# The neighbourhood attention's slots in another order on three engines, its bias table by two row tiles, and the head norm's gate moved into the slots

## The reference, cut to what matters

```python
def neighbourhood_attention(q, k, v, k_ctx, v_ctx, rpb, rows):
    # 1024 latent tokens = 16 rows of 64; 8 heads of 64; 256 context keys
    def one_row(r):
        rws = win_rows[r]                                # 8 rows of keys
        bias = rpb[:, drow[None, :, None], dcol[:, None, :]]
        s_loc = einsum(qr, kw) * scale + bias            # 16 columns of keys in each row
        s_ctx = einsum(qr, k_ctx) * scale
        p = softmax(concatenate([s_loc, s_ctx], -1))
        return einsum(p_loc, vw) + einsum(p_ctx, v_ctx)

def combine(o, na, z, dtype):
    g = head_rmsnorm(merge_heads(o), gla_norm, GLA_HEADS)      # 4 heads of 128
    return (concatenate([g, merge_heads(na)], -1) * silu(z)) @ w_out
```

## Time and profile before

| | us |
|---|---|
| median of three executions | 4608.93 |
| the profiled execution, own time | 4611.05 |
| its span (first to last instruction) | 4609.2 |
| of that, `na_block` up to its first transpose | 1909 to 1976 |
| its 32 slots | 1976 to 2255 |
| its output projection and final sums | 2255 to 2390 |
| mean granted TensorE clock over the span | 0.974 |

### The profile page before, as it was taken

How to read it: one execution, slowest core, us unless ns; L and a number is a source line. 1 busy time by engine, 2 the same in 40 slices (tenths; PEclk the granted TensorE clock), 3 DMA queues, 4 the chain that set the end, 5 groups by cost and what they waited for, 6 DMA issues and landing times. The chain is left out here.

```text
span 4609.2 us, 47596 instructions
## 1 busy us (share of the span) xinstructions
PE 4375.6 (95%) x19074; PEld 2605.8 (57%) x19074; DVE 1433.6 (31%) x3514; ACT 950.4 (21%) x1724; POOL 167.7 (4%) x225
## 2 busy tenths in 40 slices
PE   7999998999999999966889999999999989999998
PEld 3676666775547686755544467656544444444444
DVE  2236663663121455244344311111323210000002
ACT  2233332331134111233214311111111000000000
POOL 2000000000000000011011000001000000000000
PEclk9999999999999999888989999999999999999999
DMA  5310003112010111210012111112223011111110
GB/s 223 108 36 7 8 7 72 41 41 92 27 35 28 53 51 53 90 37 17 28 41 63 32 36 44 46 56 83 91 89 112 28 46 37 41 37 37 46 50 37
DMA packets 102226, 242.91 MB, mean 53 GB/s; under 512 B 15089, under 2 KB 43586, under 8 KB 100439
## 3 DMA queue, kind: packets, MB, share of 16 engines
q1 hardware_dynamic: 94968, 221.38, 14.9%
q0 software_dynamic: 5888, 13.25, 1.1%
q10 hardware_dynamic: 1152, 5.24, 0.3%
HBM read 202.78 MB, written 39.34 MB: 53 GB/s over the span
## 5 line engine op out<-in xcount | busy, mean ns | idle before, releaser
L2299 PE MATMUL lat_banks<-sbuf 128*128 128x512 f32 (+2 forms) x2368 | 846.1, 516 | 0.0
L302 PE MATMUL mlp_prod<-sbuf 128*128 128x512 f32 x1792 | 769.3, 592 | 1.5 <-DVE sbuf L375 1.5
L2299 PEld LDWEIGHTS lat_banks<-sbuf 128*128 128x128 f32 x2368 | 428.6, 206 | 377.5 <-issue 374.2
L302 PEld LDWEIGHTS mlp_prod<-sbuf 128*128 128x128 f32 x1792 | 340.4, 190 | 429.8 <-issue 428.1
L1738 PE MATMUL gla_prod<-sbuf 128*128 128x512 f32 (+1 forms) x784 | 321.4, 566 | 0.2 <-ACT sbuf L1860 0.2
L1225 PE MATMUL mls_banks<-sbuf 128*128 128x512 f32 (+1 forms) x768 | 284.3, 525 | 7.4 <-DMA sbuf<-in_l_w_in 6.8
L1738 PEld LDWEIGHTS gla_prod<-sbuf 128*128 128x128 f32 x784 | 148.0, 192 | 154.1 <-issue 146.0
L1225 PEld LDWEIGHTS mls_banks<-sbuf 128*128 128x128 f32 x768 | 144.4, 192 | 124.1 <-issue 109.1
L2519 ACT ACTIVATE sbuf<-lat_banks 128x512 f32<-128x512 f32 (+1 forms) x124 | 72.4, 583 | 680.0 <-PE lat_banks L2299 629.7
L750 PE MATMUL mla_banks<-sbuf 128*128 128x512 f32 (+1 forms) x416 | 176.0, 511 | 0.0
L351 ACT ACTIVATE sbuf<-mlp_prod 128x1024 f32<-128x1024 f32 x32 | 32.8, 1024 | 641.0 <-PE mlp_prod L302 641.0
(11 more groups left out here) (433 smaller groups left out, 5511.4 us busy)
## 6 DMA issues: line engine op xcount, KB each, us to landing
sbuf<-in_l_w_in SPq DMA_DIRECT2D x59, 512.0 KB, 3.9
sbuf<-in_w_in SPq DMA_DIRECT2D x52, 512.0 KB, 3.8
sbuf<-in_w_mlp_in SPq DMA_DIRECT2D x32, 512.0 KB, 3.6
sbuf<-in_w_mlp_out SPq DMA_DIRECT2D x32, 512.0 KB, 3.6
sbuf<-in_l_w_mod SPq DMA_DIRECT2D x12, 1024.0 KB, 11.1
sbuf<-in_l_w_mod SPq DMA_DIRECT2D x24, 512.0 KB, 5.0
scratch_gates<-sbuf SPq DMA_DIRECT2D x48, 256.0 KB, 2.9
sbuf<-scratch_gates SPq DMA_DIRECT2D x8, 1536.0 KB, 6.9
```

Source lines behind the costliest of these rows:

```text
L302: last = nc.tensor.matmul(prod[:, n % NB, o:o + 512], w[:, n % NB, k * P:(k + 1) * P], rhs, start=k == 0, stop=k == KD - 1)
L2299: last = nc.tensor.matmul(dst, lhsT, rhs, start=k == 0, stop=k == KD - 1)
```

## The change

- PE's order in the slots becomes, for each i, `turn(i)` from its third batch on, `scores(i+2)`, `weigh(i-1)`, and the first two batches of `turn(i+1)`. DVE's becomes `bias_max(i+2)`, `outputs(i-1)`, `copy(i+1)`, `inverse(i+1)`; ACT's `copy(i)`, `soft(i+1)`.
- ACT copies batches 0 and 1 of each slot, DVE 2 and 3.
- The table's 64 matmuls run as two row tiles: `hot` and `lhs` lie twice, at partitions 0 to 32 and 64 to 96, and the matmuls of the two go to different banks. There are 8 parts of 8 matmuls.
- `gla_spread` and `gla_gate` go. POOL multiplies `osum` by silu(z) (`gate(j)`, four tensor-tensor operations of 128x1024) after its second edge tile. In slots 8 to 23 (`GATE0`) `weigh` spreads two 128-token factors into free columns of its own bank, and `outputs` multiplies two 128-column pieces of `osum` with them and the gain, in one operation of 128x256.
- The fourth block of z has a place of its own in `H`, and is loaded with the others. The gates no longer stand ahead of the first slots; two of the four `gla_sums` stand behind `scores(0)`.
- `load` goes. `ones`, `ident` and `eps` are loaded at the end of `modulation`'s SP queue, and its small tensors ahead of the weights.

```diff
-            sp.dma_start(cc[:], io["cc"]).then_inc(in_sem, 16)
+            for dst, src in ((cc[:], io["cc"]), (sel[:], io["mod_sel"]), (b[:], io["l0_b_mod"]), (g[:], io["l0_norm"])):
+                sp.dma_start(dst, src).then_inc(in_sem, 16)
             for c in range(NC):
                 if c >= NB:
                     sp.wait_ge(mm_done, c - NB + 1)
                 for h in range(2):
                     sp.dma_start(w[:, c % NB, 4 * h:4 * h + 4, :],
                                  io["l0_w_mod"][(2 * c + h) * P:(2 * c + h + 1) * P, :].rearrange("p (k n) -> p k n", k=4)).then_inc(w_ready[c % NB], 16)
-                if c == 0:
-                    sp.dma_start(sel[:], io["mod_sel"]).then_inc(in_sem, 16)
-                    sp.dma_start(b[:], io["l0_b_mod"]).then_inc(in_sem, 16)
-                    sp.dma_start(g[:], io["l0_norm"]).then_inc(in_sem, 16)
+            for dst, src in ((ones, io["ones"]), (ident, io["ident"]), (eps, io["eps"])):
+                sp.dma_start(dst, src).then_inc(const_in, 16)
+            sp.wait_ge(const_in, 48)
...
+            act.wait_ge(const_in, 48)
             nc.scalar.activation(rcol[:, 0:TT], stat[:, 0:TT], ACT.Sqrt, bias=eps, scale=1.0 / D).then_inc(rooted, 1)
...
+            pe.wait_ge(const_in, 48)
             column_sums(nc, stat, total, ones, range(TT)).then_inc(ssum, 1)
...
-def load(nc, name, pairs):
...
-    on_act = [b in (1, 2) for i, b in batch]
+    on_act = [b < 2 for i, b in batch]
...
+    NO, NW, GATE0 = 8, 3, 8
...
-        hot, osq = early[0:33, 0:8192], early[:, 8192:10240].rearrange("p (a t) -> p a t", a=2)
+        hot = [early[64 * r:64 * r + 33, 0:4096] for r in range(2)]
+        osq = early[:, 4096:6144].rearrange("p (a t) -> p a t", a=2)
...
-        zg = kv[:, 1, 0:3072].rearrange("p (a t) -> p a t", a=3)
+        quarters = lambda a: a.rearrange("p (n t) -> p n t", t=256)
+        zg = [quarters(kv[:, 1, j * NLAT:(j + 1) * NLAT]) for j in range(3)] + [H[:, 0:4, 0:256]]
...
-            sp.dma_start(lhs[:], io["rpb"]).then_inc(hot_in, 16)
-            sp.dma_start(hot, io["rpb_hot"]).then_inc(hot_in, 16)
+            for r in range(2):
+                sp.dma_start(lhs[64 * r:64 * r + 33, :], io["rpb"]).then_inc(hot_in, 16)
+                sp.dma_start(hot[r], io["rpb_hot"][:, 4096 * r:4096 * (r + 1)]).then_inc(hot_in, 16)
             sp.dma_start(gl[:], io["l1_gla_norm"]).then_inc(gl_in, 16)
             load_pair(0)
-            for j in range(3):
-                sp.dma_start(zg[:, j, :], z_dram[j * P:(j + 1) * P, NCTX:T]).then_inc(zg_in[j], 16)
+            for j in range(4):
+                sp.dma_start(zg[j], quarters(z_dram[j * P:(j + 1) * P, NCTX:T])).then_inc(zg_in[j], 16)
             for j in range(4):
                 sp.dma_start(zn[:, j, :], z_dram[(4 + j) * P:(5 + j) * P, NCTX:T]).then_inc(zn_in, 16)
             sp.dma_start(gf[:], io["final_norm"]).then_inc(gf_in, 16)
             sp.dma_start(gm[:], io["g_mem"]).then_inc(gf_in, 16)
             sp.dma_start(mem, io["mem"].rearrange("p (k t) -> p k t", k=KD)).then_inc(mem_in, 16)
-            sp.wait_ge(ygla, 1)
-            sp.dma_start(zg[:, 0, :], z_dram[3 * P:4 * P, NCTX:T]).then_inc(zg_in[3], 16)
             sp.wait_ge(ygla, 4)
...
+            def gate(j):
+                pool.wait_ge(zsil, j + 1)
+                nc.gpsimd.tensor_tensor(quarters(osum[:, j, :]), quarters(osum[:, j, :]), zg[j], ALU.mult).then_inc(ygla, 1)
...
+                    if p == 0 and e == 1:
+                        pool.drain()
+                        for j in range(4):
+                            gate(j)
+                        pool.drain()
...
             def table_part(b):
-                if b >= 4:
-                    pe.wait_ge(*((tab_act, b // 2 - 1) if b % 2 == 0 else (tab_dve, b // 2 - 1)))
+
+                if b >= 2:
+                    pe.wait_ge(tab_act, b - 1)
+                    pe.wait_ge(tab_dve, b - 1)
                 for a in range(4):
                     kk = 4 * b + a
-                    last = nc.tensor.matmul(banks[:, b % 4, a * P:(a + 1) * P], hot[:, kk * P:(kk + 1) * P], lhs[:], start=True, stop=True)
+                    for r in range(2):
+                        last = nc.tensor.matmul(banks[:, 2 * (b % 2) + r, a * P:(a + 1) * P], hot[r][:, kk * P:(kk + 1) * P],
+                                                lhs[64 * r:64 * r + 33, :], start=True, stop=True)
                 last.then_inc(tabled, 1)
-
-            def gla_spread(j):
-                if j == 0:
-                    pe.wait_ge(ginv, 1)
-                else:
-                    pe.wait_ge(ygla, j)
-                for t in range(8):
-                    last = nc.tensor.matmul(banks[:, 4 + t // 4, (t % 4) * P:(t % 4 + 1) * P],
-                                            gcol[:, 8 * j + t:8 * j + t + 1].broadcast_to([P, P]), ident[:], start=True, stop=True)
-                last.then_inc(gspread, 1)
...
-                    pe.wait_ge(grooted, 1)
...
+                if 0 <= i - GATE0 < 16:
+                    pe.wait_ge(ginv, 1)
+                    for t in range(2):
+                        c = 2 * (i - GATE0) + t
+                        nc.tensor.matmul(B[:, (2 + t) * P:(3 + t) * P], gcol[:, c:c + 1].broadcast_to([P, P]), ident[:],
+                                         start=True, stop=True)
...
-            for j in range(4):
-                gla_sums(j)
-            pe.wait_ge(hot_in, 32)
-            for b in range(16):
+            gla_sums(0)
+            gla_sums(1)
+            pe.wait_ge(hot_in, 64)
+            for b in range(8):
                 table_part(b)
-            gla_spread(0)
-            scores(0)
-            for j in range(1, 4):
-                gla_spread(j)
-            scores(1)
-            for i in range(NS):
-                turn(i)
-                if i:
-                    weigh(i - 1)
+            for i in range(-2, NS + 1):
+                if 0 <= i < NS:
+                    turn(i, range(2, nb[i]))
                 if i + 2 < NS:
                     scores(i + 2)
-            weigh(NS - 1)
+                if i == -2:
+                    gla_sums(2)
+                    gla_sums(3)
+                if i >= 1:
+                    weigh(i - 1)
+                if 0 <= i + 1 < NS:
+                    turn(i + 1, range(2))
...
-                    if n == 0 and kk == 4:
+                    if n == 0 and kk == 0:
+                        pe.wait_ge(oev, 3 * NU)
+                    if n == 0 and kk == KD - 1:
                         pe.wait_ge(oev, NS)
...
+            for b in range(8):
+                table_evict(b)
+            for j in range(4):
+                act.wait_ge(zg_in[j], 16)
+                nc.scalar.activation(zg[j], zg[j], ACT.Silu).then_inc(zsil, 1)
+            act.wait_ge(zn_in, 64)
+            for j in range(4):
+                nc.scalar.activation(zn[:, j, :], zn[:, j, :], ACT.Silu)
             act.wait_ge(osum1, 4)
             nc.scalar.activation(gcol[:], banks[:, 7, 0:32], ACT.Sqrt, bias=eps, scale=1.0 / P).then_inc(grooted, 1)
-            for b in range(0, 16, 2):
-                table_evict(b)
-            for j in range(3):
-                act.wait_ge(zg_in[j], 16)
-                nc.scalar.activation(zg[:, j, :], zg[:, j, :], ACT.Silu).then_inc(zsil, 1)
-            act.wait_ge(zn_in, 64)
-            for j in range(4):
-                last = nc.scalar.activation(zn[:, j, :], zn[:, j, :], ACT.Silu)
-            act.wait_ge(zg_in[3], 16)
-            nc.scalar.activation(zg[:, 0, :], zg[:, 0, :], ACT.Silu).then_inc(zsil, 1)
             soft(0)
-            soft(1)
             for i in range(NS):
                 copy(i)
-                if i + 2 < NS:
-                    soft(i + 2)
+                if i + 1 < NS:
+                    soft(i + 1)
...
-            def gla_gate(j):
-                dve.wait_ge(gspread, j + 1)
-                nc.vector.scalar_tensor_tensor(out=osum[:, j, :], in0=osum[:, j, :], scalar=gl[:, j:j + 1],
-                                               in1=banks[:, 4:6, :].rearrange("p b t -> p (b t)"), op0=ALU.mult, op1=ALU.mult)
-                dve.wait_ge(zsil, j + 1)
-                dve.drain()
-                nc.vector.tensor_tensor(osum[:, j, :], osum[:, j, :], zg[:, j % 3, :], ALU.mult).then_inc(ygla, 1)
...
+                if 0 <= i - GATE0 < 16:
+                    j, o = divmod(2 * (i - GATE0), 8)
+                    dve.wait_ge(ygla, j + 1)
+                    x = osum[:, j, o * P:(o + 2) * P]
+                    nc.vector.scalar_tensor_tensor(out=x, in0=x, scalar=gl[:, j:j + 1], in1=B[:, 2 * P:4 * P], op0=ALU.mult, op1=ALU.mult)
...
-            for b in range(1, 16, 2):
+            for b in range(8):
                 table_evict(b)
-            dve.wait_ge(gl_in, 16)
-            dve.wait_ge(grooted, 1)
-            nc.vector.reciprocal(gcol[:], gcol[:]).then_inc(ginv, 1)
-            gla_gate(0)
-            bias_max(0)
```

(19 more changed lines are left out.)

33 lines of the change are left out of this document (11 added, 22 removed).

## The result

| | before | after |
|---|---|---|
| median of the four runs of this comparison, us | 4609.26 | 4489.75 (4487.80 to 4495.52) |
| ratio | | 0.9744, 95% interval 0.9732 to 0.9756 |
| the profiled execution, own time | 4611.05 | 4495.52 |
| its span | 4609.2 | 4493.7 |
| sums start `na_block` at | 1910.45 | 1909.09 |

The kernel is 2.6% faster. The forecast was 4480, so the gain was 119.5 us where 129 were expected; 4489.75 lies within the range of 4462 to 4522. The profiled execution was the slowest of the four, 5.8 us above their median.

What follows compares the result with a forecast made beforehand. PE was taken to bound the kernel, its pauses and low clock in the changed stage being the time to gain. Gains of 97.8 (slots), 27.7 (ahead of them) and 3.4 (start), 128.9 us, gave a median of 4480; range 4462 to 4522.

Steps and rivals of the forecast that it cites:

- The ring: In the slots, PE and DVE take turns through scores, bias, copy, transposes and weighing; PE waits 79.8 us; the change opens it.
- Rival 3: In the slots, the order does not free PE and the 2.43 us pause only moves: total 4585, chance 0.03.
- rivals 1 and 4: In the slots, the clock falls as often as now, 4501 (chance 0.14), or stays low throughout, slower, 4637 (0.03).
- each pause is paid twice: In the slots, PE loses each 2.43 us pause itself and then time at the fallen clock, 0.50.
- The slots: The 32 slots: 181.4 us against 279.2, a gain of 97.8, with 3 us for low clock; bounds 160 and 203.
- I take none for the gates' two extra changes: In the 16 gated slots, tiling changes cost nothing, only 6.9 us of passes; at 0.2 us a change, 6.4 us more.
- A slot without gates: Slots without the norm's factors: 4.95 us narrow and 5.77 wide, 10.72 a pair, 171.5 us in all.
- Ahead of the slots: Before the slots: table 13.7 us, then ACT's chain; first transpose at 1948.2 instead of 1975.9, 27.7 us earlier, bounds 30 and 14.
- The start: At the program's start, `H` issued at about 0.7 instead of 4.11 us, a gain of 3.4 us, bounds 0 and 6.
- Queues: POOL's gates (4 x 2.33 us) and the second pair's q, k, v on SP come in time for the slots.
- Everything behind the slots is as before: From the slots' end to the kernel's end, PE works without a pause and nothing changes.
- Rival 2: In the slots, DVE's copies come late behind `outputs` and `bias_max`, 1.3 us a slot, 42 us: total 4522, chance 0.12.

Runs made afterwards that it cites:

- x5: The kernel before with only the new order in the slots and the new division of copies; table, norm and start as before: 4504.21 us, ratio 0.9774.
- x2: The changed kernel without the GLA norm's factors in the slots (spreading matmuls and VectorE's multiplying operation left out): 4473.95 us, one execution.
- x1: The changed kernel with each norm factor spread by two matmuls of 64 columns, in weigh's tiling, instead of one of 128: 4483.48 us, ratio 0.9729.
- x8: The changed kernel with the next slot's first two transpose batches ahead of weigh, and factors spread by 64-column matmuls in weigh's tiling: 4501.68 us, ratio 0.9767.
- x10: x1 once more, unchanged, beside the changed kernel on the same chip: 4483.3 us, ratio 0.9730.
- x11: The changed kernel once more, unchanged, beside x10: 4484.66 us, ratio 0.9737.
- x6: The changed kernel with copies shared as before, VectorE batches 0 and 3, ScalarE 1 and 2, order unchanged: 4516.8 us, one execution.
- x7: The changed kernel with the next slot's first two transpose batches ahead of weigh instead of behind it: 4503.69 us, ratio 0.9773.

## Why the prediction was right, and where it was not

**The ring, and what opens it.** Right. The order alone took 105 us (x5), and the pause put down to DVE's copy went. Rival 3 (the order does not free PE) fell with that. The clock came back with it, 0.99 to 1.00; rivals 1 and 4 had it stay low. That "each pause is paid twice" is too strong: in the trace of before, the 32 pauses (all but one of 2.0 to 3.1 us) stand against 20 stretches at 0.50 in the slots, 68 us in all. At half speed these lose 34 us, which is what PE's busy time fell by in x5.

**The slots, 181.4 forecast, 188.4 measured.** Here lies the largest part of the error, in two terms.
- *"I take none for the gates' two extra changes."* This is the step that failed. Gates were forecast at 6.9 us and cost 13.4 (x2); the passes are 6.8, as worked out, and 6.6 is what goes when the spread takes the neighbours' tiling (x1, and 6.0 and 5.6 in x8 and x10). The prediction had the price at hand, 0.2 us a change at most from the scores' rows, or 6.4 us in all, and put it at nothing. The Trainium skill (TensorEngine Tiling, Key Properties) says that a change of tiling mode drains TensorE. The trace agrees so far as it shows a price at each change, 0.18 us on average; what TensorE does in that time it does not show.
- A slot without gates: a pair took 11.04 us in the changed kernel's trace where 10.72 was forecast. The first two batches took 1.44 us in place of 1.37 (2009.41 to 2010.85). Four transposes took from their start to the scores' 0.56 instead of 0.43 (2010.85 to 2011.41); 0.09 of that is the step into the scores' tiling (0.20 for 0.11). Six took 0.83 instead of 0.64, while the 0.16 forecast for a wide slot's fourth batch did not come. Together that is 2.5 us in 16 slots and as much again in the 16 with gates.
- Against them stand the 3 us for low clock, which the pairs above are read without, and 1 us at the ends, net of the low clock that did come (6 us at 0.72, a loss of 1.7).

**Ahead of the slots, first transpose 27.7 us earlier.** Measured from the start of the stage, 65.5 us became 37.1: 28.4. Counted so, the table began at 9.4 us for the forecast 9.1 and took 14.02 us for 13.7, at the low clock as assumed. ACT's chain set the end, and from the table's end to the first transpose it took 13.7 us where 15.0 were forecast, since the transposes waited for the first of two exponentials only. So two small misses met, and that the sum is so near is partly luck. In the second profile of the same kernel (x11) PE came to the first transpose without a pause, straight from the second scores, which ran at the low clock, and the head took the same 37.0 us: both paths are about equally long. x5 less the changed kernel gives 27.3 us for table and norm together; 13.7 of them are the table (27.67 in x5, 14.02 after), and I put the other 13.6 down to the norm's way out of the head and the order around it, which no run takes apart. In the slots the norm's way back in cost 13.4. That part of the change was thus worth almost nothing as it was made, and 7 us with x1's tiles.

**The start, 3.4 us.** `H` was issued 3.37 us earlier and ACT's wait for a small tensor ended at 9.98 us instead of 21.21, as said. The gain is 4.0 us at its place and 3.6 at the start of `na_block`, as means over profiles whose ranges overlap. That is near the forecast, but no total shows it.

**Queues.** No wait of PE on POOL or on the second pair's q, k and v appears in the slots; the gates were hidden.

**The rest.** "Everything behind the slots is as before": 2359.1 against 2354.1 in the first profile, but 2351.1 in the second of the same kernel (x11). It is no effect of the change: behind the slots the clock was at 0.50 for some 72 us in the first profile and for some 52 in the second, which at half speed is 10 us more lost, against the 8.0 us between the two. It is also 5 us of the first profile's distance from the forecast. The sum of it: slots +7.0, head -0.7, start of the stage 2.0 less gained than 3.4, tail +5.0, in all 13.3 of the 13.4 us between 4495.5 and 4482.1. Against the second median, 4484.66, the forecast of 4480 looks better than its terms are.

**Rival 2** (DVE's copies behind `outputs` and `bias_max` come late) did not occur: the only wait of PE on DVE in the slots is one of 0.6 us. x6 shows that it would have, had DVE kept the first copy, at 25 us.

## What to carry to other kernels

Where an engine waits once a round on a busy partner, draw the ring of who waits for whom, and put independent work of the next round between the two; the engine that makes room for the next batch must not have longer work ahead of that. Before moving producers ahead of a consumer, count the buffers between them: the order of x7 lost 16 us with two buffers and, against x1, won 11.5 with three. Small matmuls that slip between others should take the tiling of their neighbours.

## What the hardware showed that was not expected

- Two changes of TensorE's tiling cost 0.36 us with the same columns streamed (x1); the slots of the pairs x7 and x8, x11 and x10 differ by 6.0 and 5.6 us, 0.35 to 0.38 a gated slot. A step across a change takes 0.20 us where one within a tiling takes 0.10 to 0.11.
- Matmuls of 33 rows on two row tiles gave 0.110 us a pass alternating and 0.136 in groups of four, where one row tile gave 0.216, all at 1.2 GHz. Passes of the two tiles still started together in part when the code grouped them. PE was busy for nearly all of these stretches and the clock stayed there.
- Pauses of 0.6 to 1.45 us once in a slot left the clock at 1.00 for 180 us (x6), while pauses of 2.0 to 3.1 us had gone with 20 falls and a mean of 0.88 before.
- Code that is the same up to `na_block` reached it between 1901.5 and 1909.5 us, and left its first stage between 53.5 and 58.2. A single profile is no measure of a change worth 5 us in a kernel of this length; the stage that was changed is.
